# Transformer blocks in split fp32 on one core: the first transfers cut and reordered, VectorE's split of the first weight unit, and ten products of the identity ahead of the first matmul

## The reference, cut to what matters

```python
def rmsnorm(x, g):
    xf = x.astype(jnp.float32)
    y = xf * lax.rsqrt(jnp.mean(xf * xf, axis=-1, keepdims=True) + EPS) * g
    return y.astype(x.dtype)

# first_block
u = rmsnorm(h, norm_mix_pre[l])
z = u @ w_in[l]                       # 1024 x 4096: pool, q, k, v, gates
y_pool = pool_mixer(p, pool_w[l], pool_scale[l]) @ w_branch_pool[l]
y_attn = moba_attention(q, k, v) @ w_branch_attn[l]
m = jax.nn.sigmoid(g_pool) * y_pool + jax.nn.sigmoid(g_attn) * y_attn
h = h + rmsnorm(m @ w_out[l], norm_mix_post[l])
a = jnp.square(jax.nn.relu(rmsnorm(h, norm_mlp_pre[l]) @ w_up[l]))
h = h + rmsnorm(a @ w_down[l], norm_mlp_post[l])
# second_block: differential attention and windowed attention, each with a
# gated feed-forward block with a convolution, and a gated side input
```

## Time and profile before

| | us |
|---|---|
| median of 3 runs | 1978.21 |
| lowest and highest | 1976.29, 1978.87 |
| the profiled execution, its own time | 1979.44 |
| its span, from the first to the last instruction | 1977.6 |
| TensorE busy in the span | 1941.2 |
| ScalarE, GpSimd, VectorE busy | 925.4, 1116.3, 1183.8 |

### The profile page before, as it was taken

The page is one execution under the profiler, slowest core; times in us unless marked ns, Lnnn a source line. Parts: engine busy times, 40 slices in busy tenths (PEclk is TensorE's granted clock), DMA queues, the critical chain, the costliest instruction groups (busy, mean ns, idle before and its releaser), DMA issues.

```text
span 1977.6 us, 25179 instructions
## 1 busy us (share of the span) xinstructions
PE 1941.2 (98%) x9232; PEld 1591.5 (80%) x9232; DVE 1183.8 (60%) x1946; ACT 925.4 (47%) x1740; POOL 1116.3 (56%) x848
## 2 busy tenths in 40 slices
PE   7999999999999999999999999999999999999997
PEld 6877887888888877877888888888777888888886
DVE  6773324353433478877676646756688675746755
ACT  5653336433333356555453433445577543443443
POOL 5345545454444467454576665755784576666662
PEclk9999999999999999999999999999999999999998
DMA  4122233232232321111323222223110323222321
GB/s 160 65 70 95 87 116 127 87 112 101 96 109 96 114 89 65 53 62 56 128 98 105 96 96 96 96 91 108 66 53 33 128 96 104 98 87 96 107 93 57
DMA packets 52106, 182.72 MB, mean 92 GB/s; under 512 B 5776, under 2 KB 6160, under 8 KB 51984
## 3 DMA queue, kind: packets, MB, share of 16 engines
q1 hardware_dynamic: 51984, 181.12, 26.3%
HBM read 174.80 MB, written 6.29 MB: 92 GB/s over the span
## 4 chain that ended last, share of the span: by engine, by line
PE 92%; DVE 6%; ACT 1%; issue 1%; DMA 0%; POOL 0%; SPq 0%; DVEq 0%; ACTq 0%; POOLq 0%
PE b L393 28%; PE b L395 28%; PE b L394 28%; PE b L415 2%; PE b L407 1%; PE b L448 1%; PE b L439 1%; PE b L438 1%; DVE sm L574 1%; PE b L408 1%; PE b L409 1%; DVE ra L621 1%; DVE fa L586 0%; PE b L426 0%; DVE ra L483 0%
## 5 line engine op out<-in xcount | busy, mean ns | idle before, releaser
L239 POOL TENSOR_TENSOR ra<-raw,ra 128x512 fp32r<-128x512 f32 x632 | 881.9, 1403 | 766.0 <-ACT ra L283 762.7
L393 PE MATMUL b<-ra 128*128 128x512 f32 x2528 | 1000.8, 396 | 18.5 <-POOL ra L239 9.2
L395 PE MATMUL b<-ra 128*128 128x512 f32 x2528 | 986.2, 390 | 0.0
L394 PE MATMUL b<-ra 128*128 128x512 f32 x2528 | 985.4, 390 | 0.0
L283 ACT ACTIVATE ra<-raw 128x512 fp32r<-128x512 f32 x632 | 392.9, 628 | 537.1 <-PE b L395 534.6
L393 PEld LDWEIGHTS b<-ra 128*128 128x128 f32 x2528 | 475.5, 188 | 122.9 <-issue 15.2
L395 PEld LDWEIGHTS b<-ra 128*128 128x128 f32 x2528 | 475.2, 188 | 101.2
L394 PEld LDWEIGHTS b<-ra 128*128 128x128 f32 x2528 | 476.0, 188 | 93.5
L737 DVE TENSOR_TENSOR h<-b,h 128x512 f32<-128x512 f32 x136 | 91.7, 682 | 63.4 <-PE b L395 62.7
L628 DVE TENSOR_TENSOR tmp<-b,rb 128x512 f32<-128x512 f32 x63 | 43.2, 691 | 116.3 <-PE b L395 116.2
L621 DVE TENSOR_TENSOR ra<-b,ra 128x512 fp32r<-128x512 f32 (+4 forms) x166 | 91.8, 566 | 18.5 <-ACT ra L334 15.8
(11 more groups left out here) (276 smaller groups left out, 1902.8 us busy)
## 6 DMA issues: line engine op xcount, KB each, us to landing
raw<-in_f_g SPq DMA_DIRECT2D x40, 512.0 KB, 3.5
raw<-in_f_v SPq DMA_DIRECT2D x40, 512.0 KB, 3.5
raw<-in_f_d SPq DMA_DIRECT2D x40, 512.0 KB, 3.5
raw<-in_w_up SPq DMA_DIRECT2D x32, 512.0 KB, 3.5
raw<-in_w_down SPq DMA_DIRECT2D x32, 512.0 KB, 3.5
raw<-in_p_g SPq DMA_DIRECT2D x16, 512.0 KB, 3.5
raw<-in_w_gp SPq DMA_DIRECT2D x8, 512.0 KB, 3.5
raw<-in_w_ga SPq DMA_DIRECT2D x8, 512.0 KB, 3.4
```

What stands on the lines that cost most here:

```text
L239: e.tensor_tensor(wl, src, wh.bitcast(F), ALU.subtract).then_inc(*w_low.mark(n))
L393: e.matmul(ps, wh[:, c:c + 128], xh, start=start, stop=False)
L394: e.matmul(ps, wh[:, c:c + 128], xl, start=False, stop=False)
L395: last = e.matmul(ps, wl[:, c:c + 128], xh, start=False, stop=stop)
```

## The change

Five edits, all of them to the start.

1. Weights pair 0 comes as two transfers of one unit each (`put_first_weights`), the first of them ahead of everything else. The vectors are cut in two: the eight gain columns come third in the queue, the other 539 behind all of x. Holds on the gains stand where those on the vectors stood; a step `vectors` holds for the rest once all of x has been squared.
2. Unit 0's low part is made by VectorE (kind "split" marked "v"), not by GpSimd.
3. TensorE multiplies the identity by itself ten times into the bank of the statistics (kind "busy"), as soon as the identity is written. The results aren't used. The planner's clock of TensorE is set back to zero behind it.
4. The dates at which the planner takes x to have landed are 3.5, 5.5, 7.0 and 9.0 instead of 1.0, 3.0, 6.0 and 7.5.
5. Weights pair 2 (units 4 and 5) is issued behind the last of x. Unit 0's split is put into the table first of all, ahead of x chunk 0.

```diff
@@ sync_program
         elif kind == "weights":
-            slot, src, split_of_slot, landed = a
-            if split_of_slot is not None:
-                w.wait_ge(*split_of_slot)
-            e.dma_start(m.raw[:, slot, :, :].rearrange("p a b -> p (a b)"), src).then_inc(*landed.mark(n, 16))
+            slot, units, src, split_of_slot, landed = a
+            for t in split_of_slot:
+                w.wait_ge(*t)
+            e.dma_start(m.raw[:, slot, units, :].rearrange("p a b -> p (a b)"), src).then_inc(*landed.mark(n, 16))
@@ tensor_program
+        elif kind == "busy":
+            b, count = a
+            for q in range(count):
+                x = e.matmul(m.banks[b][:, 0:128], m.ident[:, :], m.ident[:, :], start=True, stop=True)
+            x.then_inc(*stat.mark(n))
@@ vector_program
+        elif kind == "split" and a[4] == "v":
+            src, (wh, wl), landed, unit_used, _ = a
+            w.wait_ge(*landed)
+            w.wait_ge(m.sig("w_high"), n)
+            e.tensor_tensor(wl, src, wh.bitcast(F), ALU.subtract).then_inc(*m.sig("w_low_v").mark(n))
@@ build
+    def put_first_weights(z):
+
+        name, i = plan[0]
+        sig = m.sig(f"first{z}")
+        landed_of[z] = (sig, row("weights", 0, slice(z, z + 1), A[name][i][:, S * z:S * z + S], (), sig))
 
     def put_split(u):
         k = u // 2
         slot = k % NP
-        n = row("split", m.raw[:, slot, u % 2, :], WS[u % NU], landed_of[k], unit_used.get(u - NU))
+        n = row("split", m.raw[:, slot, u % 2, :], WS[u % NU], landed_of[u], unit_used.get(u - NU), "p" if u else "v")
         done("ac", "w_high", n)
-        unit_tok[u] = done("gp", "w_low_p", n)
+        unit_tok[u] = done("gp", "w_low_p", n) if u else done("ve", "w_low_v", n)
...
+    if plan:
+        put_first_weights(0)
     h_tok = [(load(h[:, 0, :], A["x"][:, 0, :], after=0.0),)]
-    t_vec = load(vec[:, :], A["vec"], after=0.0)
+    t_gain = load(vec[:, 0:NC], A["vec"][:, 0:NC], after=0.0)
     for i, (a, b) in enumerate(((1, 2), (2, 4), (4, 6), (6, 8))):
-        if plan and i < NP:
-            put_weights(i)
-        h_tok += [(load(h[:, a:b, :], A["x"][:, a:b, :], after=(1.0, 3.0, 6.0, 7.5)[i]),)] * (b - a)
+        if plan and i == 0:
+            put_first_weights(1)
+        elif plan and i == 1:
+            put_weights(1)
+        h_tok += [(load(h[:, a:b, :], A["x"][:, a:b, :], after=(3.5, 5.5, 7.0, 9.0)[i]),)] * (b - a)
+    if plan:
+        put_weights(2)
+    t_vec = load(vec[:, NC:], A["vec"][:, NC:], after=11.0)
     t_cst = load(m.mask[:, 0:S], A["alibi"])
     n = row("constants")
     row("warm", (m.sig("elem_p"), (n, 1)))
     t_id = done("gp", "elem_p", n)
     row("hold", "pe", (t_id,))
+    done("pe", "stat_t", row("busy", STB, 10))
+    sc.clock["pe"] = 0.0
     row("hold", "dve", (t_id,))
-    row("hold", "act", (t_vec,))
-    row("hold", "dve", (t_vec,))
+    row("hold", "act", (t_gain,))
+    row("hold", "dve", (t_gain,))
@@ first_block
         u = norm(U_A, "v", -2)
+        if plan:
+            put_split(0)
+            st["split"] = 1
         launch(make_u(u, 0, ("mix_pre", 0), ()))
         while u["tok"][0] is None:
             yield "idle"
         launch(square(u, h[:, 0, :], h_tok[0][0]))
         for k in range(1, NC):
             input_of(u, k, ("mix_pre", 0), ())
+
+        def vectors():
+
+            yield 0, "v", lambda: (t_vec,) if u["n"] == NC else None
+            row("hold", "dve", (t_vec,))
+            row("hold", "act", (t_vec,))
+        launch(vectors())
```

More of the change, by code:

```diff
@@ L234, in gpsimd_program @@
                             pattern=[[-1, 128]], channel_multiplier=1).then_inc(*els.mark(n))
-        elif kind == "split":
-            src, (wh, wl), landed, unit_used = a
+        elif kind == "split" and a[4] == "p":
+            src, (wh, wl), landed, unit_used, _ = a
             w.wait_ge(*landed)
@@ L921, in build @@
     st = dict(split=0, used=0)
-    slot_split = [None] * NP
+    slot_split = [()] * NP
     unit_tok = {}
@@ L931, in put_weights @@
         sig = m.sig(f"raw{slot}")
-        landed_of[k] = (sig, row("weights", slot, A[name][i], slot_split[slot], sig))
+        landed_of[2 * k] = landed_of[2 * k + 1] = (sig, row("weights", slot, slice(0, 2), A[name][i], slot_split[slot], sig))
+    def put_first_weights(z):
+        name, i = plan[0]
+        sig = m.sig(f"first{z}")
+        landed_of[z] = (sig, row("weights", 0, slice(z, z + 1), A[name][i][:, S * z:S * z + S], (), sig))
     def put_split(u):
@@ L936, in put_split @@
         slot = k % NP
-        n = row("split", m.raw[:, slot, u % 2, :], WS[u % NU], landed_of[k], unit_used.get(u - NU))
+        n = row("split", m.raw[:, slot, u % 2, :], WS[u % NU], landed_of[u], unit_used.get(u - NU), "p" if u else "v")
         done("ac", "w_high", n)
-        unit_tok[u] = done("gp", "w_low_p", n)
+        unit_tok[u] = done("gp", "w_low_p", n) if u else done("ve", "w_low_v", n)
         if u % 2:
-            slot_split[slot] = unit_tok[u]
+            slot_split[slot] = (unit_tok[u - 1], unit_tok[u])
             if k + NP < len(plan):
```

## The result

The changed kernel is slower: 1982.98 us median of 7 runs (1981.86 to 1985.51) against 1978.21 (1974.96 to 1978.87, 7 runs). The ratio is 1.0028, with a 95% interval of 1.0019 to 1.0037. The forecast was 1979.5, no difference that can be told; the time came out near the upper end of the range, where the forecast had put the rival in which the clock falls (1982.9). That its figure and the median agree to 0.1 us is luck: of its terms the shift was too small, the price of the clock too large and the base another one, as the part on why the prediction was wrong works out.

The account below looks back on a forecast made before the run. TensorE was taken to bound the kernel, busy 98% of the span. Late statistics delay line 448, swallowing the earlier start: +1.3 us on 1979.44 gives 1980.7, put on the median as 1979.5; range 1975.5 to 1983.2.

Parts of the forecast that it names:

- the rival in which the clock falls: TensorE's clock falls in the new wait at line 448: +4.7 us in all, 1982.9; chance 0.27.
- the price of the clock: Cost of a fall at line 448: 0.9 us for that line plus 2.5 for 12 matmuls at the lower clock.
- the base: Profiled execution's 1979.44 us gave 1980.7; the forecast was moved onto the median of 1978.21, giving 1979.5.
- the landing of x chunks 2 and 3: These chunks come into use at 9.66 us instead of 10.31, having 0.27 MB less ahead of them.
- the sum: Line 448 starts at about 26.9 instead of 25.56, all earlier gains spent waiting: +1.3 us, clock kept.
- What bounds the start: TensorE is busy 98% of the span; the change can act only in the first 30 us, through its waits or clock.
- the slack: Before line 448: the sum of squares was ready 1.14 us before TensorE wanted it; statistics 2.5 us later would eat this.
- the turns of VectorE and GpSimd: Before line 448: the two exclude each other, so VectorE's eight operations take 1.70 us each beside GpSimd's low parts.
- Clock kept or fallen: At line 448's new wait of 3.4 to 4.2 us: clock kept, chance 0.53, or fallen, chance 0.27.
- The argument against it: Against a fall at line 448: thin work preceded the fall at the trace's end, but full matmuls stand ahead here.
- The other support: For the clock holding: earlier TensorE waits of up to 2.4 us left the page's clock at 9 or more tenths.
- The start: First matmul at 7.25 us, 1.9 earlier than 9.18, with ScalarE starting at 4.87; no effect on the time in the end.

Follow-up runs that it names:

- e1: The changed kernel with the planner's dates of x set back to 1.0, 3.0, 6.0 and 7.5: 1977.98 us, ratio 1.0002 to the kernel before.
- e2: The kernel before with only the dates of x changed to 3.5, 5.5, 7.0 and 9.0: 1982.45 us, ratio 1.0027.
- e4: The changed kernel without the ten products of the identity ahead of the first matmul: 1982.93 us, ratio 1.0029 to the kernel before.
- e8: The changed kernel with the vectors whole in one transfer, third in the queue: 1983.16 us, ratio 1.0031 to the kernel before.
- e12: The changed kernel with the first pair of weights whole in one transfer, ahead of everything: 1982.41 us, ratio 1.0024 to the kernel before.
- e11: The kernel before with only the dates of x changed to 1.0, 7.0, 7.5 and 7.5: 1978.93 us, ratio 1.0004.
- e3: The changed kernel with fourteen more products of the identity right ahead of line 448: 1982.14 us, ratio 1.0021 to the kernel before.
- e5: The changed kernel with the old dates of x and sixteen products of the identity in place of ten: 1978.53 us, ratio 1.0003 to the kernel before.
- e7: The changed kernel, new dates kept, with line 448 twelve matmuls later in TensorE's order: 1980.22 us, ratio 1.0015 to the kernel before.

## Why the prediction was wrong, point by point

Two steps failed: the landing of x chunks 2 and 3, which cost 0.9 us in line 448, and the clock, which the sum took as kept, at no cost, and whose fall cost 1.7. The trace's shift of 3.1 us is the 1.3 of the sum, these two, and 0.9 given back near 45 us. The other 1.7 us up to the difference of the medians, 4.8, is the base, last below.

- **What bounds the start, the slack, the turns of VectorE and GpSimd: right.** VectorE's eight operations took a turn each (1.7 us from start to start, from the second on), the last addition decided line 448, and e1 and e2 show that the dates alone, by the order that they set, are the whole cause of the loss. From the landing to the last addition I had 17.2 us; it was 16.95 (10.83 to 27.78).
- **The landing of x chunks 2 and 3: the term that was mis-sized.** The step "by the same lead they land now 0.27 MB earlier ... so at 9.66" failed. It was 10.83 here, 10.1 to 11.5 in the traces with the same transfers, and the test with 0.27 MB more ahead of it did not move it. So the bytes ahead in the queue don't set it by themselves: the step kept the old rate up to the landing, 271 GB/s, and its lead of 0.41 MB, and here the rate was 256 and the lead 0.67 MB (2.77 less 2.10). Why the rate fell and why landings scatter stays open. Line 448 came at 27.83 and not at 26.9, and the shift there was +2.3 and not +1.3.
- **Clock kept or fallen: the wrong case was held the likelier** (0.53 against 0.27). In the five traces with a wait at line 448 (2.0 to 4.0 us: the changed kernel, e2, e4, e8, e12) the clock fell each time; behind the 0.93 of e11 it held. The argument against it, that full matmuls stand ahead here and thin work did at the end of the trace, didn't hold: in e4 and e12 the clock fell inside the wait, straight behind full matmuls. The other support was a misreading. The page's clock of 9 or more tenths is a mean over slices of 49 us, in which a fall of 3 us can't be seen; the trace of before itself has one at 1523.6, behind a wait of only 1.57 us, while its waits of 2.4 and 1.9 us left the clock at 1.00. The price was over-estimated, 3.4 us, and is 1.7 in this trace (0.4 in line 448, 1.3 behind it), since the clock came back after six matmuls and not twelve. In e4 and e12, where it was down before line 448 began, it was 2.5 and 2.8.
- **The wait near 45 us** (0.9) was not in the sum; it went, in this trace, and made the loss smaller.
- **The start: 7.25 expected, 7.75 found**, by the landing of the gains (5.49 for 4.87; 4.5 to 5.0 in eight other traces with the same cuts). As forecast this had no effect on the time. That chunk 2 waits for unit 2 was forecast (14.4), and e3, e5 and e7 show that this wait is itself long enough for a fall.
- **The base.** The sum stood against 1979.44 and I moved it onto the median. Trace against trace the change costs 3.0 us, median against median 4.8: the profiled execution of before lies 1.2 us above its median, that of the changed kernel 0.5 below. The fall near 1523 isn't the difference, since both traces paid it. The slow start may be a part: the first twelve matmuls took 5.25 us in the trace of before (9.18 to 14.43) and 4.35 in that of e11 (9.80 to 14.15). With one trace of each kernel the rest stays open.

## What to carry to other kernels

Where a planner's dates decide the order, compare the order and look for an engine's gap that closes: a pause of GpSimd can be what lets VectorE keep a chain on time. Size the slack of the next consumer before valuing an earlier start, and count a TensorE pause of 2 us as 2 us plus, in a part of the runs, some 1.5 more for a fall of the clock. Look for such falls in the granted clock of short stretches right behind the waits, not in the slices of the page. A gain of 1 to 2 us at the start could not be shown here by medians of 11 runs, when single executions differ by 1.5 us at one place.

## What was not expected of the hardware

- The clock fell behind a wait of 2.05 us ahead of the short products of line 448 (e2), and behind waits of 1.9 and 1.6 us at 331 and 1523 in some traces and not in others, 1.5 to 1.6 us each time. The Trainium skill (TensorE: Matmul & The Clock Gate, HAM oscillation — how this bites in real kernels) warns of longer gaps; the granted clock of 0.50 behind these shows that shorter ones were enough.
- Ten products of 128 columns in plain fp32 took 3.93 us here and 4.6 us in traces where the clock stayed low through them, so 0.46 each. In this trace the clock rose during them (their records go 0.21 apart up to 4.5 us and 0.11 behind it), where without them (e4) the weights' matmuls still went 0.43 apart up to 12 us; but the pause of 2.30 us behind them lost it again.
- Transfers of the same list landed up to 1.4 us apart from one trace to the next (x chunk 2 in use at 10.06 in e1 and 11.50 in e7).
- The list with the first pair and the vectors cut moved 246 to 257 GB/s up to that landing, and 271 to 279 with one of them or both whole.
